# Who builds the tap diagonals and who sums which taps of a depthwise convolution, in a two-block transformer kernel on one core

## The reference, cut to what matters

```python
def conformer_conv(h, w_in, b_in, w_dw, b_dw, ln_g, ln_b, w_out):
    u = h @ w_in + b_in
    a, gt = jnp.split(u, 2, axis=-1)
    u = a * jax.nn.sigmoid(gt)
    y = lax.conv_general_dilated(            # depthwise, causal, 31 taps
        u, w_dw[:, None, :], window_strides=(1,),
        padding=[(CONV_WIDTH - 1, 0)],
        dimension_numbers=('NWC', 'WIO', 'NWC'),
        feature_group_count=D_MODEL) + b_dw
    y = jax.nn.silu(layernorm(y, ln_g, ln_b))
    return (y @ w_out).astype(h.dtype)
```

## Time and profile before

| | us |
| --- | --- |
| median of 3 runs | 966.71 (965.07 to 967.89) |
| the profiled execution, device time | 966.98 |
| its span in the profile | 965.1 |

### The profile page before, as it was taken

One profiled execution on the slowest core, in us unless ns is written; L12 is line 12 of the kernel. 1 busy time (PEld: TensorE's weight loads), 2 busy tenths in 40 slices (PEclk: granted clock), 3 DMA queues, 4 the chain that ended last, 5 costly groups with the idle time before them and its releaser, 6 DMA issues.

```text
span 965.1 us, 13242 instructions
## 1 busy us (share of the span) xinstructions
PE 908.6 (94%) x5176; PEld 537.3 (56%) x5176; DVE 279.2 (29%) x738; ACT 207.0 (21%) x496; POOL 196.6 (20%) x327
## 2 busy tenths in 40 slices
PE   4999998999999999989889888999999999999996
PEld 3788686554443443434334334487766558688544
DVE  2399724310101111010010010134035336260334
ACT  2355514210000000000000000032215511011540
POOL 0187300121111111111011010032003201023221
PEclk9999999999999999999999999999999999999999
DMA  9997975689999999999999999991400934402001
GB/s 362 426 430 287 383 285 218 234 349 428 429 426 431 425 429 426 429 426 429 426 431 426 426 429 423 430 373 50 175 2 1 399 146 164 173 2 88 1 1 43
DMA packets 22522, 286.12 MB, mean 296 GB/s; under 512 B 2498, under 2 KB 3266, under 8 KB 4930
## 3 DMA queue, kind: packets, MB, share of 16 engines
q1 hardware_dynamic: 21744, 283.99, 70.9%
q10 hardware_dynamic: 722, 1.33, 0.4%
HBM read 284.26 MB, written 1.05 MB: 296 GB/s over the span
## 4 chain that ended last, share of the span: by engine, by line
PE 68%; DMA 20%; DVE 8%; issue 2%; POOL 1%; ACT 1%; SPq 0%; POOLq 0%; DVEq 0%; ACTq 0%
DMA arena<-in_w_expert_up 19%; PE bank L969 17%; PE bank L1205 16%; PE bank L1222 6%; DVE bank L1662 5%; PE bank L1415 5%; PE bank L1232 3%; PE bank L1362 3%; PE bank L1017 1%; PE bank L1193 1%; PE bank L1548 1%; PE bank L1394 1%; PE bank L1379 1%; PE bank L1446 1%; PE bank L1458 1%
## 5 line engine op out<-in xcount | busy, mean ns | idle before, releaser
L1205 PE MATMUL bank<-arena 128*64 128x512 f32 x1024 | 226.1, 594 | 24.0 <-DMA arena<-in_w_expert_up 24.0
L969 PE MATMUL bank<-arena 128*128 128x256 f32 (+1 forms) x992 | 211.1, 374 | 1.7 <-ACT arena L821 1.4
L969 PEld LDWEIGHTS bank<-arena 128*128 128x128 f32 x992 | 183.5, 190 | 27.9 <-issue 4.5
L1205 PEld LDWEIGHTS bank<-arena 128*64 128x64 f32 x1024 | 79.0, 137 | 167.2 <-issue 167.0
L1222 PE MATMUL bank<-arena 128*64 128x512 f32 x512 | 116.9, 599 | 0.8 <-ACT arena L791 0.8
L1862 DVE TENSOR_TENSOR arena<-bank,arena 64x512 f32<-64x512 f32 x32 | 21.8, 682 | 277.6 <-ACT arena L787 277.5
L791 ACT ACTIVATE arena<-bank 128x512 f32<-128x512 f32 x32 | 19.1, 597 | 386.1 <-PE bank L1214 386.1
L1222 PEld LDWEIGHTS bank<-arena 128*64 128x64 f32 x512 | 34.1, 136 | 65.8 <-issue 65.8
L550 POOL COPY der<-arena 128x4 f32 (+1 forms) x30 | 5.6, 187 | 318.4 <-PE bank L1214 298.4
L1232 PE MATMUL bank<-arena 64*128 64x256 f32 x512 | 65.8, 387 | 0.8 <-DVE arena L1865 0.8
L1662 DVE SCALAR_TENSOR_TENSOR bank<-arena,par,bank 128x256 f32<-128x256 f32 x143 | 58.3, 483 | 0.6
(11 more groups left out here) (252 smaller groups left out, 834.3 us busy)
## 6 DMA issues: line engine op xcount, KB each, us to landing
arena<-in_w_expert_down SPq DMA_DIRECT2D x32, 2048.0 KB, 31.6
arena<-in_w_expert_gate SPq DMA_DIRECT2D x31, 2048.0 KB, 25.9
arena<-in_w_expert_up SPq DMA_DIRECT2D x31, 2048.0 KB, 30.4
arena<-in_w_ada SPq DMA_DIRECT2D x12, 2048.0 KB, 31.0
arena<-in_w_kv SPq DMA_DIRECT2D x4, 2048.0 KB, 15.7
arena<-in_w_in_b SPq DMA_DIRECT2D x4, 2048.0 KB, 8.1
arena<-in_w_glu SPq DMA_DIRECT2D x3, 2048.0 KB, 36.2
arena<-in_w_uq SPq DMA_DIRECT2D x4, 1152.0 KB, 15.5
```

What stands on the lines that cost most here:

```text
L969: mm = pe.matmul(bank[part:part + m, at:at + n], w[:, k, lo:lo + m], rhs[:, k0 + k, :], start=(k == 0), stop=(k == tiles - 1))
L1205: mm = pe.matmul(GU_BANK[half * WIN:(half + 1) * WIN, :], xw[b][:, k, :], w[:, k, :], start=(k == 0), stop=(k == KD - 1), skip_group_check ...
```

## The change

ACT builds the diagonals in place of POOL. It builds those of PE's first chunk ahead of `sigmoid(0)`, and those of each next chunk in the middle of a chunk's products: after `sigmoid(j + 1)` and before the fifth product. The ring of eight and its wait on `diag_used` stay. POOL_TAPS goes from nine to ten per chunk (eight to nine in the last). PE_TAPS falls from three to two in chunks 0 to 3 and stays otherwise; in chunks 4 to 7 DVE has one tap fewer.

```diff
-PE_TAPS = (3, 3, 3, 3, 3, 3, 3, 5)
-POOL_TAPS = (9, 9, 9, 9, 9, 9, 9, 8)
+PE_TAPS = (2, 2, 2, 2, 3, 3, 3, 5)
+POOL_TAPS = (10, 10, 10, 10, 10, 10, 10, 9)
@@ gpsimd
-            made, added = 0, 0
+            added = 0
             for c in range(KD):
-                j = PE_ORDER[c]
-                for w in range(PE_TAPS[j]):
-                    if made >= DIAGS:
-                        pool.wait_ge(sem("diag_used"), made - DIAGS + 1)
-                    pool.tensor_scalar(diag[:, made % DIAGS, :], ident, col("conv_w_dw", w * KD + j), 0.0,
-                                       ALU.mult, ALU.add).then_inc(sem("diag_ready"), 1)
-                    made += 1
                 total_ = pool_sum[:, c % SUMS, :]
@@ gpsimd
-            pool.wait_ge(sem("diag_used"), made)
+            pool.wait_ge(sem("diag_used"), sum(PE_TAPS))
@@ scalar
+            diags = [0]
+
+            def diagonals(c):
+
+                for w in range(PE_TAPS[PE_ORDER[c]]):
+                    m = diags[0]
+                    if m >= DIAGS:
+                        act.wait_ge(sem("diag_used"), m - DIAGS + 1)
+                    act.activation(diag[:, m % DIAGS, :], ident, ACT.Copy,
+                                   scale=col("conv_w_dw", w * KD + PE_ORDER[c])).then_inc(sem("diag_ready"), 1)
+                    diags[0] += 1
+
+            act.wait_ge(sem("consts_in"), 16)
+            diagonals(0)
             sigmoid(0)
             for j in range(KD):
                 before = 4 if j < KD - 1 else 2
@@ scalar
                     sigmoid(j + 1)
                 else:
                     ada_row(4, 0, 2)
+                if j < KD - 1:
+                    diagonals(j + 1)
                 products(j, before, POOL_TAPS[j])
```

## The result

The changed kernel takes 973.87 us (median of six, 972.47 to 976.48), against 967.25 for the kernel before in the same six rounds: a ratio of 1.0071, with a 95% interval of 1.0051 to 1.0091. By the ratio it is slower by 6.9 us, give or take 1.9; the two medians are 6.6 apart. The forecast was 974.0, with a range of 971.5 to 977.0.

The account below looks back on a forecast made before the run. It took DVE, PE and POOL as level in the convolution stage; ACT's waits for the ring delay chunk 7's last sum from 107.5 to 114.5, so 966.98 + 7.0 = 974.0, with a range of 971.5 to 977.0.

Parts of the forecast that it names:

- What bounds the stage: Convolution stage: DVE and PE level at 97.5, POOL level at the end; relieving one engine alone buys nearly nothing.
- Unit costs: Per-instruction times: PE matmul 0.43, POOL add 0.85, ACT product 0.40, ACT diagonal 0.31, DVE tap saved 0.2 to 0.4.
- Step 1: Chunk 4: ACT waits 4.8 for a tap of `convolve(3)`; fourth add at 83.9, sum at 89.0, was 82.4.
- Step 2: Chunk 5's late first add delays `sigmoid(6)` to 90.3; DVE merges chunk 6 at 90.8 instead of 89.00.
- Step 3: Diagonals 16 to 18 wait for `convolve(4)`'s taps until 91.6; chunk 5's fourth add at 92.5, sum at 97.6.
- Step 4: DVE merges chunk 7 at 99.45 (was 97.02), `convolve(7)` starts at 100.2 (was 97.75), PE idle 4.8.
- Steps 5 and 6: Chunk 6's fourth add at 102.6, PE idle 3.7 before the columns; chunk 7's sum at 114.5, was 107.52.
- the clock rival: PE's clock halves in the new idle times, adding 1.3 to 2.0 to the 7.0: 975.3 to 976.0; chance 0.33.
- Absorption: Expert loop: loads follow PE, so the whole 7.0 stays; rival says 2.5 is won back, 971.5, chance 0.09.
- Rival "not slower": Convolution stage: the ring's wait is hidden in POOL's slack of 7 us, at most 0.3 shorter, 966.7; chance 0.08.
- the 4.8: Expected PE idle time before `convolve(7)`, weighed between 6.49 (clock fell) and 2.53 (clock kept).

Follow-up runs that it names:

- ring16: The changed kernel with a ring of 16 diagonals in place of 8, in a new place: 964.86 us, ratio 0.9986 to the kernel before.
- filler: The changed kernel with nine unused PE matmuls ahead of `convolve(7)` and six ahead of the columns: 973.18 us, ratio 1.0067 to the kernel before.
- ring11: The changed kernel with a ring of 11 diagonals in place of 8, in a new place: 965.21 us, ratio 0.9986 to the kernel before.
- filler9: The changed kernel with only the nine unused PE matmuls ahead of `convolve(7)`: 976.24 us, ratio 1.0090 to the kernel before.
- act_diags_old_split: The changed kernel with the old PE_TAPS and POOL_TAPS, ACT still building the diagonals: 974.11 us, ratio 1.0071 to the kernel before.
- pool_diags_new_split: The kernel before with the new PE_TAPS and POOL_TAPS, POOL still building the diagonals: 969.04 us, ratio 1.0029 to the kernel before.
- ring10: The changed kernel with a ring of 10 diagonals in place of 8, in a new place: 972.39 us, ratio 1.0057 to the kernel before.
- diags_behind: The changed kernel with each chunk's diagonals behind its last product, ring still at 8: 966.97 us, ratio 0.9999 to the kernel before.

## Why the prediction was right

**What bounds the stage.** Right. DVE, PE and POOL are level before, and a saving on PE alone ends as idle time (1.69 in ring16).

**Unit costs.** A diagonal takes 0.39 on ACT and two take 0.68, so 0.29 from start to start, where I took 0.31. POOL's adds are 0.85 apart in the changed kernel, as I had it ((7.51 - 0.73) / 8, with 0.73 for one), but 0.87 before ((6.83 - 0.73) / 7): dividing a group's time by its count hid that. The DVE taps were put at 0.2 to 0.4 and measured at 0.26.

**Steps 1 to 4.** Each stands in the profile after, within 0.2 except for the wait's length. Step 1: `convolve(3)` at 81.96 (81.9), the fourth add of chunk 4 at 83.90 (83.9). The wait is 5.46 in place of 4.8, because ACT reached it at 77.1 and not 77.8; its end is set by PE, so that changed nothing. It ends at the first tap of `convolve(3)`, which frees the fourth diagonal (82.59), and the second tap frees the fifth at about 83.0. The prediction names the second tap, but its 4.8 reaches only to the first. Step 2: sigmoid of chunk 6 at 90.11 (90.3), merge at 90.67 (90.8). Step 3: 92.53 (92.5). Step 4: merge of chunk 7 at 99.31 (99.45), `convolve(7)` at 100.05 (100.2).

**Steps 5 and 6.** Here the forecast and the trace part, by the clock alone. The fourth add of chunk 6 came at 103.87 instead of 102.6, the last sum at 103.87 + 11.86 = 115.73 instead of 114.5, the mean at 116.32 instead of 115.1. The difference is 1.2 to 1.3, three taps at half rate, as the clock rival had it. PE's second idle time shrank with it, from the 3.7 expected to 2.42, since the slow taps filled it, and the clock did not fall again (1.00 from 106 on). So what the stage did is that rival with one fall (7.0 + 1.3), not the forecast; I had given the rival 0.33 and the forecast 0.48. With the clock held up (`filler`) the steps' own sum of 7.0 measures 6.8.

**The rule of the Trainium skill** (TensorE: Matmul & The Clock Gate, section "Why this matters for your kernels") against long idle gaps speaks for that rival, and the trace agrees: the clock was at half behind 4.42 us of idle. The length of the idle time alone does not decide, as the last section shows.

**Absorption.** Right that the loads follow PE: PE starts its first expert at 177.64 against 169.44, 8.20 later, and it is still 8.20 later at the sixteenth. PE's timeline after:

```profile
177.64 7.09 PE L1214 MATMUL bank<-arena 128*64 128x512 f32 x32
...
379.74 7.04 PE L1214 MATMUL bank<-arena 128*64 128x512 f32 x32
394.10 7.09 PE L1214 MATMUL bank<-arena 128*64 128x512 f32 x32 [1.20 <-DMA arena<-in_w_expert_up]
...
637.30 10.60 PE L978 MATMUL bank<-arena 128*128 128x256 f32 x48 [1.45 <-ACT arena L830]
```

The group at 379.74 was at 371.54 before, the one at 637.30 at 630.46: in the stretch bound by loads 1.4 is given back, 459.66 from the first expert to the attention stage in place of 461.02. Is that absorption? Over the twelve profiles this length is 459.6 to 462.0: ring16 459.59 and ring11 462.04, whose stages are alike to 0.02, and filler9 461.82, whose stage is among the longest. It goes neither with the length of the stage nor with its end. So it is spread from run to run in the stretch bound by loads, and in the profiled pair it happened to hide the clock's 1.4. The totals follow the stage: over the eleven kernels the loss by the ratio and the loss of the distance differ by at most 1.3, in both directions, while the losses run from -2.0 to 8.1. In the totals the changed kernel's loss is 6.9 with an interval of 4.9 to 8.8, which holds both 7.0 and the stage's 8.1. So the mechanism of steps 1 to 4 was right and the stage was 1.2 too short in the sum; that the total came out on 974.0 all the same is luck. The runs do not show whether a longer series would settle 1 us above it.

**Rival "not slower".** Its point of decision, the last sum ready by 107.6, was the right one to watch. ring11 meets it with one change, three places more in the ring: its last add ends at 92.91 + 11.86 = 104.77.

## What to carry to other kernels

When work moves from one engine's program to another's, its waits move with it. Ask at the new place what is queued behind each wait, and which event the wait needs there: a ring of eight was deep enough between two chunks and three places too shallow in the middle of one. A sum of busy times would have given a loss of the same size here for the wrong reason, so test the wait (a ring twice as large, the call a few lines lower) before trimming work. One or two places more can mislead: the ring of 10 took back 3.0 of the 8.1, and up to 1.4 of that is the clock, which did not fall there; the eleventh place took back the rest. And measure by the distance between two events of the changed stage where the total scatters by more than the effect.

## What the runs showed of the hardware

TensorE's clock falls after shorter idle times than I had looked for, and not by their length alone. It was at 0.50 behind 4.42 us of idle (changed kernel), 3.55 (`act_diags_old_split`), 3.48 (`filler9`) and even 2.30 (`pool_diags_new_split`), but stayed at 1.00 behind 3.57 (`ring10`) and 2.53. PE was dense ahead of all of them in this stage. The fall need not come in the idle time either: in the changed kernel it came 2.5 into it, in `pool_diags_new_split` at about 100, when PE had been at work again since 99.17. The two kernels whose idle times and clocks contrast most, columns as in rows 7, first of `pool_diags_new_split` and then of `ring10`:

```profile
100.00:102.00 2.00, 2.00 (x7) 1.57 (x6) 2.00 (x6) 1.22 (x3) 1.57 (x4) 0.52 1.00 393
```

```profile
100.00:102.00 2.00, 2.00 (x11) 1.73 (x11) 2.00 (x6) 1.70 (x4) 1.38 (x2) 1.00 0.94 369
```

In the same two microseconds the one issues 7 tap instructions and the other 11. What decides between them was not tried.

The kernel before had such a case already, and the prediction misread it. It put the half rate of the eight instructions at 18.82 down to the 6.49 us of idle ahead of 12.11, but right ahead of them lie 1.78 us of idle, and the clock fell only when they had started. The kernel before, columns as in rows 7:

```profile
18.00:18.50 0.50, 0.00 (x0) 0.00 (x0) 0.46 (x3) 0.42 (x1) 0.00 (x0) 1.00 0.90 369
19.00:22.00 3.00, 3.00 (x8) 2.19 (x7) 0.15 (x1) 0.00 (x0) 0.00 (x0) 0.50 1.06 452
```

So a fall close to 1.8 us of idle, though with PE less busy ahead of it than in the stage, stood in the trace when the 4.8 was weighed, and the rival deserved more than 0.33. The recorded clock is to be read together with durations: in `diags_behind` it is 1.00 from 18 to 24, yet the same eight instructions, at 18.92, took 3.75.
